# Five gated one-hot columns in one VectorE instruction each, and gate maps read back a quarter of the tiles at a time, in a two-layer decoder kernel

## What is computed

```python
q = (h @ wq).reshape(B, S, 8, 2, 128)
scores = einsum('bshcd,hcnd->bshcn', q, subkeys)       # 8 heads, two halves, 128 keys each
s_top, i_top = top_k(scores, 16)                       # 16 keys of each half
cand = s_top[..., 0, :, None] + s_top[..., 1, None, :] # 256 sums
best, pos = top_k(cand, 16)                            # the 16 best pairs
expert_idx = i_a * 128 + i_b                           # of 16384 experts
gates = softmax(best)
a = einsum('cd,ced->ce', hh, u[expert_idx])            # 128 experts for each token
act = gelu(a) * gates
out = einsum('ce,ced->cd', act, v[expert_idx])
```

## Time and profile before

| | |
|---|---|
| median of three runs | 3956.79 us (3955.44 to 3960.62) |
| profiled execution | 3953.5 us, its span 3950.8 us |
| TensorE busy | 3538.9 us, 90% of the span |
| VectorE busy | 2597.2 us, 66% |
| GpSimd busy | 1437.0 us, 36% |
| ScalarE busy | 1106.9 us, 28% |
| mean granted TensorE clock | 0.945 of full speed |

### The profile page before, as it was taken

How to read it: one execution, slowest core, us unless ns; L and a number is a source line. 1 busy time by engine, 2 the same in 40 slices (tenths; PEclk the granted TensorE clock), 3 DMA queues, 4 the chain that set the end, 5 groups by cost and what they waited for, 6 DMA issues and landing times.

```text
span 3950.8 us, 50789 instructions
## 1 busy us (share of the span) xinstructions
PE 3538.9 (90%) x13822; PEld 2271.9 (58%) x13822; DVE 2597.2 (66%) x5393; ACT 1106.9 (28%) x2531; POOL 1437.0 (36%) x1220
## 2 busy tenths in 40 slices
PE   4998998999866999998978889989997689999987
PEld 2554445776754448873445544467776544688633
DVE  7555116998877777676555640288998777766675
ACT  1333112322395003330023330123235920133100
POOL 0000002444434565566500000044444356556673
PEclk9999999999967999999989999999998789999999
DMA  6322225888756999999952222178886579999997
GB/s 243 128 99 75 77 79 182 321 314 304 271 157 218 401 402 387 344 383 390 384 197 101 96 80 101 54 265 321 300 312 237 160 297 405 396 364 370 384 385 312
DMA packets 278111, 1016.48 MB, mean 257 GB/s; under 512 B 31353, under 2 KB 48249, under 8 KB 266881
## 3 DMA queue, kind: packets, MB, share of 16 engines
q0 software_dynamic: 157696, 570.50, 38.5%
q1 hardware_dynamic: 120194, 443.42, 29.7%
HBM read 988.63 MB, written 25.17 MB: 257 GB/s over the span
## 4 chain that ended last, share of the span: by engine, by line
PE 47%; DVE 23%; DMA 9%; issue 7%; ACT 7%; DVEq 5%; POOL 2%; ACTq 1%; SPq 0%; POOLq 0%
PE ps L605 16%; PE ps L784 8%; PE ps L558 6%; DMA arena<-in_u_dram,idx 5%; DVE mod L1423 4%; DVE arena L1417 4%; ACT mod L950 3%; DVE arena L1207 3%; ACT mod L946 2%; PE ps L516 2%; PE ps L493 2%; DMA arena<-in_v_dram,idx 2%; PE ps L613 2%; PE ps L548 2%; PE ps L637 1%
## 5 line engine op out<-in xcount | busy, mean ns | idle before, releaser
L1166 POOL DMA_INDIRECT arena<-in_u_dram,idx x512 | 670.0, 1309 | 978.0 <-issue 658.5
L558 PE MATMUL ps<-hT,mod 128*128 128x256 f32 x4096 | 928.4, 380 | 0.0
L605 PE MATMUL ps<-arena 128*128 128x512 f32 x2048 | 889.4, 597 | 31.2 <-DVE arena L1467 27.4
L1166 POOL DMA_INDIRECT arena<-in_v_dram,idx x512 | 648.3, 1266 | 642.6 <-DVE mod L1423 380.4
L558 PEld LDWEIGHTS ps<-hT,mod 128*128 128x128 f32 x4096 | 760.8, 191 | 93.3
L1417 DVE CUSTOM_DVE_ANT_0 arena<-arena 128x1024 f32<-128x1024 f32 x512 | 616.7, 1224 | 245.4 <-DMA arena<-in_u_dram,idx 242.0
L1423 DVE SCALAR_TENSOR_TENSOR mod<-arena,mod 128x1024 f32<-128x1024 f32 x512 | 657.2, 1284 | 135.9 <-DMA arena<-in_v_dram,idx 107.9
L605 PEld LDWEIGHTS ps<-arena 128*128 128x128 f32 x2048 | 392.2, 192 | 525.9 <-issue 525.8
L978 ACT COPY mod<-ps 128x512 f32<-128x512 f32 x512 | 274.7, 590 | 555.6 <-PE ps L548 555.6
L548 PE MATMUL ps<-const,arena 128*128 128x128 f32 x2048 | 269.0, 275 | 21.7 <-ACT mod L978 20.9
L548 PEld LDWEIGHTS ps<-const,arena 128*128 128x128 f32 x2048 | 239.1, 141 | 52.8 <-ACT mod L978 28.3
(11 more groups left out here) (202 smaller groups left out, 3611.8 us busy)
## 6 DMA issues: line engine op xcount, KB each, us to landing
arena<-in_u_dram SPq DMA_DIRECT2D x256, 512.0 KB, 6.9
arena<-in_v_dram SPq DMA_DIRECT2D x256, 512.0 KB, 6.9
arena<-in_ada_w_dram SPq DMA_DIRECT2D x56, 1024.0 KB, 5.4
hT<-gate_scratch POOLq DMA_DIRECT2D x128, 256.0 KB, 10.0
arena<-in_w_qkv_dram SPq DMA_DIRECT2D x48, 512.0 KB, 6.1
arena<-in_w_m_dram SPq DMA_DIRECT2D x16, 1536.0 KB, 6.8
arena<-in_w_q_dram SPq DMA_DIRECT2D x32, 576.0 KB, 6.3
gate_scratch<-hT SPq DMA_DIRECT2D x64, 256.0 KB, 2.1
```

The costliest lines, as they stand in the source:

```text
L558: last = pe.matmul(ps[:, 6 + tile // 2 % 2, tile % 2 * NT:(tile % 2 + 1) * NT], u_turned[:, tile % 2, k * P:(k + 1) * P], hT[:, k, DT0:SEQ ...
L605: last = pe.matmul(ps[:, 2 * c + n, :], act_t[:, e, c * P:(c + 1) * P], stream[:, slot, n * 512:(n + 1) * 512], start=(half == 0 and e == ...
L1166: pool.indirect_dma_start(out=ring[:, r % RING, :], out_offset=None, in_=table, in_offset=bass.IndirectOffsetOnAxis(ap=idx[:, j % 4, k:k + ...
```

## The change

Three edits. VectorE now writes the gated one-hot columns of five tokens of a batch, in one instruction for each token (compare with the row number, times the gate, both taken from a column of one number per partition); ScalarE writes three instead of six. The order in which a kept map lies in its slot and in DRAM is changed, so that the gates of tiles 0 to 31 of all 8 tokens lie together, and those of tiles 32 to 63. And each read brings the 128 KB that its pass uses, instead of 256 KB.

```diff
-P_ACT = 6
+P_ACT = 3
...
-                act.copy(kept[slot].rearrange("p a (t i) -> p a t i", t=4),
-                         ps[:, bank:bank + 2, :].rearrange("p a (t i) -> p a t i", t=4)[:, :, :, HALF:2 * HALF]
+                act.copy(kept[slot].rearrange("p h (t i) -> p t h i", t=BATCH),
+                         ps[:, bank:bank + 2, :].rearrange("p a (t h i) -> p (a t) h i", t=4, h=4)[:, :, 2:4, :]
                          ).then_inc(S["gs_done"], 1)
...
-                    pool.dma_start(kept[slot], gate_dram[:, r, :].rearrange("p (a n) -> p a n", a=2)).then_inc(kept_in[slot], 16)
+                    pool.dma_start(kept[slot][:, half, :], gate_dram[:, r, half * NT:(half + 1) * NT]).then_inc(kept_in[slot], 16)
...
-            def q_batch(l, b):
+            def columns(l, b):
...
-                p = p1[:, s, P_ACT * P:BATCH * P].rearrange("p (t i) -> p t i", t=n)
-                dve.tensor_tensor(p, iota[:, :].unsqueeze(1).broadcast_to([P, n, P]),
-                                  pqgT[:, 1, rest].unsqueeze(2).broadcast_to([P, n, P]), ALU.is_equal)
                 dve.tensor_tensor(q1[s].rearrange("p (t i) -> p t i", t=BATCH),
                                   iota[:, :].unsqueeze(1).broadcast_to([P, BATCH, P]),
-                                  pqgT[:, 0, of].unsqueeze(2).broadcast_to([P, BATCH, P]), ALU.is_equal)
-                dve.drain()
-                dve.tensor_tensor(p, p, pqgT[:, 2, rest].unsqueeze(2).broadcast_to([P, n, P]),
-                                  ALU.mult).then_inc(S["q_done"], 1)
+                                  pqgT[:, 0, BATCH * b:BATCH * (b + 1)].unsqueeze(2).broadcast_to([P, BATCH, P]), ALU.is_equal)
+                for t in range(P_ACT, BATCH):
+                    n = BATCH * b + t
+                    last = dve.tensor_scalar(p1[:, s, t * P:(t + 1) * P], iota[:, :], pqgT[:, 1, n:n + 1], pqgT[:, 2, n:n + 1],
+                                             ALU.is_equal, ALU.mult)
+                last.then_inc(S["q_done"], 1)
...
-                acts = act_t[:, 32 * part:32 * part + 32, BATCH * r:BATCH * (r + 1)].rearrange("p e (a t) -> p e a t", a=2)
-                gate = kept[slot].rearrange("p a (t i) -> p i a t", t=4)[:, 32 * part:32 * part + 32]
+                acts = act_t[:, 32 * part:32 * part + 32, BATCH * r:BATCH * (r + 1)]
+                gate = kept[slot][:, part, :].rearrange("p (t i) -> p i t", t=BATCH)
```

More of the change, by code:

```diff
@@ L1425, in rows @@
                         dve.drain()
-            def q_batch(l, b):
-                s, n = b % 2, BATCH - P_ACT
-                of, rest = slice(BATCH * b, BATCH * (b + 1)), slice(BATCH * b + P_ACT, BATCH * (b + 1))
+            def columns(l, b):
+                s = b % 2
                 dve.wait_ge(S["g_done"], NB * l + b + G_START - 1)
                 park()
-                p = p1[:, s, P_ACT * P:BATCH * P].rearrange("p (t i) -> p t i", t=n)
-                dve.tensor_tensor(p, iota[:, :].unsqueeze(1).broadcast_to([P, n, P]),
-                                  pqgT[:, 1, rest].unsqueeze(2).broadcast_to([P, n, P]), ALU.is_equal)
                 dve.tensor_tensor(q1[s].rearrange("p (t i) -> p t i", t=BATCH),
                                   iota[:, :].unsqueeze(1).broadcast_to([P, BATCH, P]),
-                                  pqgT[:, 0, of].unsqueeze(2).broadcast_to([P, BATCH, P]), ALU.is_equal)
-                dve.drain()
-                dve.tensor_tensor(p, p, pqgT[:, 2, rest].unsqueeze(2).broadcast_to([P, n, P]),
-                                  ALU.mult).then_inc(S["q_done"], 1)
+                                  pqgT[:, 0, BATCH * b:BATCH * (b + 1)].unsqueeze(2).broadcast_to([P, BATCH, P]), ALU.is_equal)
[4 more added lines that the diff above has]
+                last.then_inc(S["q_done"], 1)
             def gate_batch(l, b):
@@ L1454, in gate_maps @@
                 for b in range(NB):
-                    q_batch(l, b)
+                    columns(l, b)
                     if b >= 1:
```

## The result

The changed kernel is faster, by 1.75%. It takes 3884.88 us (median of 4 runs, 3882.48 to 3890.02), beside 3956.11 us (4 runs, 3950.5 to 3960.62) for the kernel before. The ratio is 0.9825, with a 95% interval of 0.9812 to 0.9837. The profiled execution took 3883.4 us (its span 3881.7), 70.1 us less than the profiled one of before. The forecast had 61.9 us less and 3895 us, with a range of 3875 to 3933.

A forecast was written before the change was run, and what follows sets the result against it. Most of the span was taken as TensorE's own work, so only its waits could give: 28.6 us in the gate maps plus 33.3 at the kept maps' stops, 61.9 less, giving 3895 us, range 3875 to 3933.

The forecast's parts named there:

- VectorE's turn: Gate maps: VectorE sets a turn of 4.36 us on average, instead of ScalarE's 4.81, at 0.26 us per column.
- dear: Rival, gate maps: columns cost 0.346 us each or GpSimd holds them up, so little is gained; 3920 us, chance 22%.
- cheap: Rival, gate maps: columns cost only 0.20 us each, a turn 0.3 us less; 3877 us, chance 8%.
- The gate maps: Moving columns from ScalarE to VectorE shortens this stage by 14.3 us a layer, 28.6 us in both.
- The first value tiles: Stage behind the gate maps: it only shifts with their end, its own length changing by 0.
- The kept maps: Halved reads shorten both passes, removing TensorE's stop before tile 32 in each layer; 33.3 us gained in all.
- One sign: Sign of being right: the kept maps and rows land in under 10 us.
- Line 1467, now 1465: VectorE's multiplication in the second pass over kept maps: the new order may speed it up, but was costed at nothing.
- The reading of the order: Gate maps: GpSimd's instruction waits through VectorE's columns, so the new ones make it wait and cost nothing.
- the prediction's signs of being wrong: Gate maps: among them, new instructions over 0.4 us or with gaps, GpSimd's instruction ending before them.
- The 0.36 us a turn: Gate maps: loss if GpSimd's instruction came first and held up the columns, 11.5 us a layer; within a 22% rival.
- only just: Gate maps: TensorE's eight pairs, 3.78 us at the lower clock plus some 0.2 handing over, still fit in 4.2.

The follow-up runs named there:

- e5: The changed kernel with four columns written by ScalarE and four by VectorE, instead of three and five; 3874.62 us, ratio 0.9793.
- e6: The changed kernel with two columns written by ScalarE and six by VectorE, instead of three and five; 3898.96 us in a single run.
- e2: The kernel before with only the kept maps' new order and 128 KB reads, ScalarE still writing six columns; 3945.1 us, ratio 0.9945.
- e7: The changed kernel with 24 rows in the gate maps instead of 32, the others consumed right behind; 3851.84 us, ratio 0.9742.
- e3: The changed kernel with the new order of the kept maps, but each read bringing the whole 256 KB again; ratio 0.9909.
- e4: The changed kernel with VectorE's five column instructions ahead of the comparison instead of behind it; ratio 0.982.
- e9: e7 with four columns on ScalarE instead of three; ratio 0.9748 of the kernel before.

## Why the prediction was right, and where its sizes were off

1. **VectorE's turn.** Right, to 0.03 us. Forecast, by its terms: 4.53 with a row of `v` and 4.19 with one of `u`. Measured: 4.50 and 4.16, the five columns 1.28 from start to start. The price of a column of 0.26, read from a form at 346 ns less an overlap of 0.09, came out in e5, the changed kernel and e6 alike. The rivals "dear" (0.346 or held) and "cheap" (0.20) both fall.

2. **The gate maps.** The mechanism was right and the size 3.4 and 2.4 us too small. For layer 0: the 29 plain turns make 125.1 us instead of 139.5, 14.4 less (forecast 13.0; of the 1.4 that it fell short, 0.9 are the 0.03 a turn, the rest comes from two short turns, the first with 3.97 us and the one behind `unit_gates` with 3.46). The first batch starts 4.6 us behind line 576 instead of 6.4, 1.8 less (forecast 1.9). The `unit_gates` turn is 6.78 instead of 8.01, 1.2 less (0.9). The `topk` turn is 14.27 instead of 12.99, 1.3 more (1.5). A term that the sum left out is the tail: from the last batch to the first value tile it was 5.45 us and is 3.88, 1.6 less. In the earlier trace rows the last batch took 3.59 us, at the lower clock, and now it takes 2.02, at the higher one (its row above); the difference of 1.57 is the 1.6. The terms are 14.4 + 1.8 + 1.2 - 1.3 + 1.6 = 17.7. That the last batch met the higher clock is not a thing that the change makes sure of: in layer 1 it took 2.61 us, and the tail was 1.0 shorter.

3. **The first value tiles.** Costed at nothing, they took 1.7 us less in layer 0 (221.5 to 219.8) and no less in layer 1 (221.5 to 221.6). The 1.7 us sit at the very start of the stage. Where it takes 221.5 us, some of its first matmuls take 0.85 us from start to start and not 0.43, at TensorE's lower clock: the fourth to sixth and a part of two more in layer 0 before, where the granted clock over the first 14 us is 0.88, and the first four in layer 1 of the changed kernel (0.87). In layer 0 of the changed kernel it is 1.00 and none is slow. The last batch of the gate maps does not decide it: in both layers of e2 it took 3.61 us and the stage 219.8, and in layer 1 of e7 2.02 and 221.5. So it hangs on whether the clock happens to be at its lower level when the value tiles begin, and is not a gain to be counted on. Layer 1 of e6 even took 3.1 us more (222.9).

4. **The kept maps.** The stops go, as forecast, and so the gain is what they had cost: 16.65 and 16.95 us (forecast 16.5 and 16.8). The size could hardly come out otherwise once the pass ends in time; what the forecast had to get right was the turn. The ways there were a little off. A turn of pass 2 went from 2.91 to 2.47 us ((100.1 - 10)/31 and (86.6 - 10)/31), forecast 2.4; one of pass 1 from 2.69 to 2.26, forecast 2.35. Pass 2 ends 13.9 us before it is needed in layer 0 and 12.6 in layer 1; the forecast was 26 us earlier where 13.4 suffice, so 12.6. One sign was not met in full: the landing was to be under 10 us, and it is 7.7 for the maps but 10.0 for the rows of `u`. How much of the shorter turn is bytes and how much GpSimd's shorter instruction stays open (e3).

5. **Line 1467, now 1465.** Costed at nothing, and rightly: the new order gives nothing back. The medians of the passes are 600 and 608 ns in layer 0 before, 604 to 609 after.

6. **GpSimd and the columns.** The reading of the order was half right. GpSimd's instruction does meet the columns and they cost nothing for it, but it does not wait through all five (that it would end before them was among the prediction's signs of being wrong): it ends 0.89 us behind the start of the columns (1103.62 and 1102.73), so just after the fourth has begun. In a turn with a row of `v` it took about 1.75 us before, takes 1.40 now, and 0.93 with the columns first. The Trainium skill ("SBUF — State Buffer", section "Who interferes with whom") says that of a tensor-scalar in its two-port mode and a GpSimd instruction, the one that issues first gets the shared port pair for its whole instruction, and the other fully blocks. Neither order shows that in full: of the columns that began under GpSimd's instruction only one was longer, up to its end (340 ns grew to 430 in the changed kernel and to at most 550 in e4), those ahead of it kept their usual 328 to 345 ns, the next instruction started on time, and the turn grew by 0.03 in e4. Whether these columns ran in the two-port mode at all is in no trace here. The 0.36 us a turn was not paid.

7. **TensorE at its lower clock** was said to fit "only just", and does at three columns on ScalarE: a batch of 3.75 us lengthens neither the 4.50 turn nor the 4.16 one. The next steps give less than a column a turn: in e5 because ScalarE ends last in the turns with a row of `u`, and in e9, as I read it, because of the loop.

8. **Three readings of the rows were off, and cost the sum nothing.** The prediction lets every batch of TensorE wait for line 950. The one behind `topk` does not: the earlier trace rows has it with "issue" (1233.09). It counts three places where TensorE waits in each layer, and works out two. And it puts GpSimd's instruction 0.3 us behind a row. In the earlier trace rows the row ends at 1102.94 (0.20 before 1103.14) and GpSimd starts at 1103.78, 0.84 behind it; the 0.3 is its distance from the start of line 1436.

## What to carry to other kernels

Cost a chain of short instructions from start to start, with the overlap read from their neighbours; the mean duration of 0.34 would have been a third more than the 0.26 that a column costs here. When work is moved from the engine that sets the turn to its neighbour, ask at once what else lies in the neighbour's turn that needn't be there: moving eight rows and the `topk` that hung on them behind the stage took another 0.8% off, more than half of it by the `topk`, where the columns themselves had taken 34 of 3956 us, 0.9%. And keep an account of the margin that a fix leaves: 13.9 us here, of which the first such step left about 1. Last, the releaser that a trace names is not always the one that counts: compare the ends of all that a wait needs with its end.

The version with 24 rows in the gate maps (e7) beats both kernels: 3851.84 us, 0.9742 of the kernel before. Since the changed kernel is at 0.9825, with intervals that don't touch, e7 is 0.8% faster than it.

## What the runs showed of the hardware

- A tensor-scalar instruction of 128 columns with two per-partition operands lasts 327 to 341 ns, and in a row of its kind the next starts 0.26 us behind it. Beside GpSimd's indirect DMA instruction, which began first, one of five lasts up to 433 ns (changed kernel) or 550 (e4) and ends 0.05 us behind it. Those ahead of it, under the same instruction, do not last longer, and the next instruction starts on time.
- In a turn with a row of `v`, GpSimd's indirect DMA instruction took about 1.75 us beside the comparison, a drain and line 1440 (before), 1.40 beside the comparison and the short columns (after), and 0.93 where it began under the short columns (e4). It starts 0.83 us behind the end of VectorE's row in all three.
- GpSimd's read instruction took 0.76 us for 256 KB in two runs per partition (before and e3) and 0.58 for 128 KB in one (after).
- With the gate maps 17 us shorter and the same matmuls, TensorE's granted clock there rose from 0.68 to 0.78. Single batches take 2.02 us at the higher level and 3.75 at the lower, and matmuls of line 605 0.43 and 0.85.
- Line 1465 reads both operands from SBUF, 256 elements, and takes 607 ns, as line 1467 did with the other order of the gates (604). In both orders its neighbouring reads of the gates lie apart in the slot (32 numbers after, 64 before), where line 1440, 0.42 us for as many elements, reads neighbours and one repeated number. Whether that is the reason no run shows.
